# A chunked recurrence inside a two-block transformer kernel: crossed block products, convolution taps on two other engines, and three moved steps

## The reference

```python
y = _rwkv7_scan(stack(rh, rh), stack(w_f, w_b), stack(k_f, k_b), stack(vh, vh),
                stack(-kk, -kk), stack(b_f, b_b)).swapaxes(0, 1)
...
def _conformer_conv(u, dw_w, dw_b, ln_g, ln_b):
    h = u[..., :CV_WIDTH] * jax.nn.sigmoid(u[..., CV_WIDTH:])
    h = lax.conv_general_dilated(h, dw_w[:, None, :], (1,), [(CV_CONV_LEN // 2, CV_CONV_LEN // 2)],
                                 dimension_numbers=('NWC', 'WIO', 'NWC'),
                                 feature_group_count=CV_WIDTH) + dw_b
    return jax.nn.silu(_layernorm(h, ln_g, ln_b))
```

## Time and profile before

| | us |
|---|---|
| median of three runs | 2925.84 (2919.92 to 2928.39) |
| the profiled execution | 2918.31 |
| its span in the trace | 2916.2 |
| chunk loop of layer 0, first product of group 0 to the end of group 3 | 288.78 to 399.60 |
| chunk loop of layer 1 | 1054.24 to 1156.00 |

### The profile page before, as it was taken

One profiled execution on the slowest core, in us unless ns is written; L12 is line 12 of the kernel. 1 busy time (PEld: TensorE's weight loads), 2 busy tenths in 40 slices (PEclk: granted clock), 3 DMA queues, 4 the chain that ended last, 5 costly groups with the idle time before them and its releaser, 6 DMA issues.

```text
span 2916.2 us, 50739 instructions
## 1 busy us (share of the span) xinstructions
PE 2723.9 (93%) x21324; PEld 2292.6 (79%) x21324; DVE 1932.3 (66%) x2283; ACT 1478.5 (51%) x1753; POOL 103.4 (4%) x79
## 2 busy tenths in 40 slices
PE   6998888999999978799999999999999789989999
PEld 4875876888768767778878787887877779987999
DVE  3365865322454666488888888888888657665766
ACT  3345243222334433377677677767776445443544
POOL 1100000000013000100000000000000000000000
PEclk9998999999999999899999999999999889999999
DMA  8514101322234230189899898989996424542453
GB/s 320 220 58 168 74 3 58 116 88 101 91 130 170 86 125 4 40 333 371 336 348 352 334 367 335 369 337 349 364 346 258 163 102 174 188 149 87 159 188 116
DMA packets 81796, 581.69 MB, mean 199 GB/s; under 512 B 9272, under 2 KB 11072, under 8 KB 11840
## 3 DMA queue, kind: packets, MB, share of 16 engines
q1 hardware_dynamic: 78336, 571.48, 52.2%
q10 hardware_dynamic: 3264, 7.33, 0.7%
HBM read 577.73 MB, written 1.05 MB: 198 GB/s over the span
## 4 chain that ended last, share of the span: by engine, by line
PE 81%; DVE 9%; ACT 4%; PEld 2%; issue 1%; DMA 1%; PEldq 1%; POOL 0%; POOLq 0%; ACTq 0%; DVEq 0%; SPq 0%
PE banks L2496 20%; PE banks L2520 11%; PE banks L1077 8%; PE banks L857 8%; PE banks L2836 8%; PE banks L1103 3%; PE banks L891 3%; PE banks L3164 3%; PE banks L1540 3%; PE banks L2088 1%; DVE ring_split L307 1%; PEld banks L679 1%; DVE ring_split L2673 1%; PE banks L522 1%; DVE x_buf L2662 1%
## 5 line engine op out<-in xcount | busy, mean ns | idle before, releaser
L2673 DVE TENSOR_TENSOR ring_split<-ring,arena_split 128x2048 fp32r<-128x2048 f32 x336 | 768.2, 2291 | 90.9 <-ACT arena_split L2601 83.2
L2601 ACT ACTIVATE arena_split<-ring 128x2048 fp32r<-128x2048 f32 x336 | 644.4, 1919 | 52.3 <-PE banks L2520 52.3
L307 DVE TENSOR_TENSOR ring_split<-ring,arena_split 128x2048 fp32r<-128x2048 f32 x144 | 331.1, 2301 | 346.4 <-ACT arena_split L301 346.4
L301 ACT ACTIVATE arena_split<-ring 128x2048 fp32r<-128x2048 f32 x144 | 274.4, 1908 | 104.4 <-PE banks L1077 74.0
L2496 PE MATMUL banks<-arena_split 128*128 128x512 f32 x896 | 300.7, 398 | 11.7 <-DVE ring_split L2673 11.7
L2496 PE MATMUL banks<-arena_split,mix_split 128*128 128x512 f32 x896 | 304.2, 401 | 6.4 <-DVE ring_split L2673 6.4
L2520 PE MATMUL banks<-arena_split 128*128 128x512 f32 x896 | 297.4, 392 | 1.0 <-DVE arena_split L2702 1.0
L2496 PEld LDWEIGHTS banks<-arena_split 128*128 128x128 f32 x896 | 169.1, 189 | 48.8 <-DVE ring_split L2673 13.4
L2496 PEld LDWEIGHTS banks<-arena_split,mix_split 128*128 128x128 f32 x896 | 168.3, 188 | 45.0 <-DVE ring_split L2673 8.3
L2520 PEld LDWEIGHTS banks<-arena_split 128*128 128x128 f32 x896 | 168.2, 188 | 43.2 <-issue 4.0
L857 PE MATMUL banks<-mix_split,ring_split 128*128 128x256 f32 x704 | 199.0, 283 | 0.0
(11 more groups left out here) (408 smaller groups left out, 5431.9 us busy)
## 6 DMA issues: line engine op xcount, KB each, us to landing
ring<-parts SPq DMA_DIRECT2D x541, 1024.0 KB, 4.8
arena<-bias ACTq DMA_DIRECT2D x2, 2048.0 KB, 9.7
x_buf<-xt SPq DMA_DIRECT2D x1, 2048.0 KB, 7.8
constants<-con SPq DMA_DIRECT2D x1, 1952.0 KB, 14.5
out<-x_buf ACTq DMA_DIRECT2D x4, 256.0 KB, 2.2
arena<-lora ACTq DMA_DIRECT2D x2, 256.0 KB, 3.2
arena<-gate ACTq DMA_DIRECT2D x2, 256.0 KB, 3.5
arena<-sgw ACTq DMA_DIRECT2D x2, 256.0 KB
```

Of the source, the lines that this page charges most:

```text
L301: act.activation(high[:, m % depth, :], slots[:, n % RING, :], ACT.Copy).then_inc(w_high.h, w_high.one(times))
L307: dve.tensor_tensor(low_slots[:, n % RING, :], slots[:, n % RING, :], high[:, m % high.shape[1], :].bitcast(F32), ALU.subtract).then_inc(w ...
L2601: act.activation(high[:, m % 3, :], slots[:, m % RING, :], ACT.Copy).then_inc(wh_ok.h, 1)
L2673: dve.tensor_tensor(low_slots[:, m % RING, :], slots[:, m % RING, :], high[:, m % 3, :].bitcast(F32), ALU.subtract).then_inc(wl_ok.h, 1)
```

## The change

It has five parts.

1. **Crossed block products.** D2T.D2, D2.E, D2.D2T, D4T.D4, D4.E, LL.E and E.LL (steps p2, p3, p5) go through `crossed`, which puts the second direction's output into the other partition half and into the next bank. What is added to E (`E + D2.E`, `E + D4.E`) can no longer be added by VectorE, because E lies in the old half, so `plus=True` adds E on TensorE, as a product with the identity into the same accumulation; VectorE then copies. The order of blocks in DD, DT, LL, E changes from step-first to direction-first. `apply` (the two solves) crosses too.
2. **Taps.** In layer 0, channel tile 0, VectorE keeps taps 0 to 15 (16 instructions). All the others become a product on ScalarE (`Taps.products`) into a small ring of buffers and an addition on GpSimd (`Taps.sums`): 45 of 512 columns in layer 0, with 2 buffers; 60 of 256 columns in layer 1, with 4. ScalarE waits for GpSimd when the ring is full.
3. **The next group's `dl`** runs on TensorE between `solve(s, 1)` and `p7`, and VectorE masks it (`grams_out`) ahead of `g`. `bs` now waits for the mask `l` of the next group.
4. **Low weight halves.** The first is cut in four quarters that VectorE does inside group 3; the second moves into the tail, behind the first state update. ScalarE's high halves stay.
5. **The ring of tap buffers** lies over three tables that only the second block uses (`cos`, `sin`, `sel`, 1024 columns, 512 KB). They are no longer loaded at the start, but by SyncE ahead of the experts' first weights. `kb1` moves from before p3 to before p4.

The core of the diff:

```diff
+        def products(self, act, count):
+            made, added = S("cv_part"), S("cv_tap")
+            for n in range(self.made, min(self.made + count, len(self.units))):
+                i, t = self.units[n]
+                if n >= len(self.parts):
+                    act.wait_ge(added.h, added.at(n - len(self.parts) + 1))
+                act.activation(self.parts[n % len(self.parts)], self.source(i, t), ACT.Copy, scale=Q1(self.l, "cv_w", 2 * t + i))\
+                    .then_inc(made.h, made.one())
...
+        def sums(self, pool):
+            for n, (i, t) in enumerate(self.units):
...
+                pool.wait_ge(made.h, made.at(n + 1))
+                pool.tensor_tensor(self.acc[i], self.acc[i], self.parts[n % len(self.parts)], ALU.add).then_inc(added.h, added.one())
...
+            def crossed(b, k, left, right, plus=False):
+                o = [bank(b + d)[:, k * 256:(k + 1) * 256].rearrange("p (i t) -> p i t", i=4) for d in range(2)]
+                for i in range(4):
+                    for w in range(2 if plus else 1):
+                        for d in range(2):
+                            for h in hs:
+                                to = hs[1 - hs.index(h)] if d else h
+                                mm = pe.matmul(o[d][to, i, :], eye[h, 0, :] if w else left[h, 4 * d + i, :], right[h, 4 * d + i, :],
+                                               start=w == 0, stop=w == int(plus))
...
-                products(b8(0), D2T, D2)
-                products(b8(1), D2, D2T)
-                products(b8(2), D2, E[g % 2]).then_inc(P_.h, P_.one(f"p2_{g}"))
+                crossed(0, 0, D2T, D2)
+                crossed(0, 1, D2, E[g % 2], plus=True)
+                pe.wait_ge(V_.h, V_.at(f"km0_{g}"))
+                crossed(2, 0, D2, D2T).then_inc(P_.h, P_.one(f"p2_{g}"))
                 if g:
                     solve(s, 0)
-                pe.wait_ge(V_.h, V_.at(f"km0_{g}"))
-                against_zr(kt, g, 1).then_inc(P_.h, P_.one(f"kb1_{g}"))
...
-                products(b8(0), D4T, D4)
+                crossed(2, 0, D4T, D4)
                 pe.wait_ge(V_.h, V_.at(f"e2_{g}"))
-                products(b8(1), D4, E[g % 2]).then_inc(P_.h, P_.one(f"p3_{g}"))
+                crossed(0, 0, D4, E[g % 2], plus=True).then_inc(P_.h, P_.one(f"p3_{g}"))
                 if g:
                     state(s, 0)
+                pe.wait_ge(A_.h, A_.at(f"d8_{g}"))
+                against_zr(kt, g, 1).then_inc(P_.h, P_.one(f"kb1_{g}"))
...
-                products(b8(0), LL, E[g % 2])
-                products(b8(1), E[g % 2], LL).then_inc(P_.h, P_.one(f"p5_{g}"))
+                crossed(2, 0, LL, E[g % 2])
+                crossed(0, 0, E[g % 2], LL).then_inc(P_.h, P_.one(f"p5_{g}"))
...
                 if g:
                     solve(s, 1)
+                if g + 1 < NG:
+                    grams(g + 1)
...
+                if g + 1 < NG:
+                    pe.wait_ge(V_.h, V_.at(f"l_{g + 1}"))
                 turned((0, 1), 0, lambda h, q, cs: bt[h, q, cs], g).then_inc(P_.h, P_.one(f"bs_{g}"))
...
+                taps.products(act, 2 if taps.own else 2)
+                pair_out("n", "p5", g, 0, N1)
...
-                if g >= NG - 2:
-                    split_low(dve, out_high, out_first + g - (NG - 2), 2 + g - (NG - 2))
...
                     state(NG - 1, 0)
+                    split_low(dve, out_high, out_first + 1, 3)
...
+            late = slice(CON["cos"][0], CON["sel"][1])
+            sp.dma_start(con[:, late], con_in[:, late]).then_inc(S("rotation_loaded").h, 16)
```

More of the change, by code:

```diff
@@ new lines, in begin @@
+        def begin(self, act):
+            first = S("cv_begun")
+            for i in range(1 if self.own else 0, 2):
+                act.activation(self.acc[i], self.source(i, 0), ACT.Identity, scale=Q1(self.l, "cv_w", i), bias=Q1(self.l, "cv_b", i))\
+                    .then_inc(first.h, first.one())
+        def products(self, act, count):
[6 more added lines that the diff above has]
+                    .then_inc(made.h, made.one())
+            self.made = min(self.made + count, len(self.units))
@@ L1667, in _ @@
                 mm.then_inc(P_.h, P_.one(f"dl_{g}"))
+            grams(0)
+            for g in range(NG):
+                s = g - 1
                 if g:
@@ L1824, in _ @@
                 fill_act(act, g, "zb")
+                taps.products(act, 1 if taps.own else 2)
                 out("d2t", "p1", g, 2, D2T)
@@ L1828, in _ @@
                 fill_act(act, g, "p1")
-                out("d4t", "p2", g, 1, D4T)
+                taps.products(act, 2 if taps.own else 3)
+                pair_out("d4t", "p2", g, 2, D4T)
                 if g:
@@ L1838, in _ @@
                 fill_act(act, g, "p4")
-                out("n", "p5", g, 1, N1)
+                taps.products(act, 2 if taps.own else 2)
+                pair_out("n", "p5", g, 0, N1)
                 if g:
@@ L1842, in _ @@
                 fill_act(act, g, "p5")
-                out("n2", "p6", g, 3, N2)
+                taps.products(act, 1 if taps.own else 2)
+                out("n2", "p6", g, 4, N2)
                 if g:
@@ L1952, in _ @@
                 after(f"p2_{g}")
-                copy(D4, b8(0), f"d4_{g}")
-                add(e, b8(2), e, f"e2_{g}")
+                copy(pair_like(D4), pair(0, 0), f"d4_{g}")
+                copy(pair_like(e), pair(0, 1), f"e2_{g}")
+                taps.some(dve, 1)
+                after(f"p3_{g}")
+                copy(pair_like(e), pair(0, 0), f"e3_{g}")
+                if g:
+                    state(s, 0)
                 after(f"kb1_{g}")
@@ L1957, in _ @@
                 taps.some(dve, 1)
[L1958 to L1963 removed]
+                if g == NG - 1:
+                    quarter_low(0)
                 after(f"p4_{g}")
                 own()
[L1966 removed]
+                add(e, b8(0), e, f"e4_{g}")
                 taps.some(dve, 1)
+                if g == NG - 1:
+                    quarter_low(1)
                 after(f"p5_{g}")
[L1969 to L1970 removed]
+                copy(pair_like(NTb), pair(2, 0), f"nt_{g}")
+                add(pair_like(INT_), pair(2, 0), eye_pair, f"int_{g}")
+                if g + 1 < NG:
+                    grams_out(g + 1)
+                else:
+                    quarter_low(2)
+                    quarter_low(3)
                 taps.some(dve, 2)
```

139 lines of the change are left out of this document (87 added, 52 removed).

## The result

| | us |
|---|---|
| the kernel before, median of 12 runs | 2924.66 (2918.43 to 2929.32) |
| the changed kernel, median of 12 runs | 2931.88 (2925.17 to 2939.85) |
| ratio changed to before, 95% interval | 1.0023 (1.0014 to 1.0032), +6.7 us |
| its profiled execution, span | 2939.85, 2938.0 |

What follows compares the result with a forecast made beforehand. No one engine bounds it: a relay of TensorE batches and copies does. Layer 0 4.0 + layer 1 6.0 + stall 8.4 - GpSimd contention 5 = 13.4, rounded to 14 us: median 2925.8 to 2912, range 2901 to 2924 (forecast's own 2906 to 2917).

Steps and rivals of the forecast that it cites:

- The price of a crossed product: Matmul records using all four quadrants: 17 ns each taken, 22 as a bound, 30 as the worst; uncrossed 30 to 31.
- The legs: Start-to-start steps in both loops: gains of 4.0 us in layer 0 and 6.0 us in layer 1.
- p3's reader to p4: Leg in each group: 0.74 us becomes 1.1 behind `kb1`, a loss of 0.4, or 0.15 in layer 0.
- p4 to p5: Leg of 2.45 us in layer 1, TensorE's own work 2.0: gain 0.4 in groups 1 and 2; 0 where outputs run.
- reader to p6: Leg after p5: 0.75 us both ways if ScalarE's `n` is punctual; `n` 0.5 late in layer 0, 0.1 in layer 1.
- The early `dl`: From p6 onwards: replaces TensorE idle time, so gains nothing; `bs` waits at most 0.3 us for the mask `l`.
- The stall at group 3: Group 3 of both layers: TensorE's wait during VectorE's low half and the lower clock after it go, gain 8.4 us.
- GpSimd against VectorE: Both loops: the engines stop each other, costing 4 us in layer 0 and 1 in layer 1; loss 5, between 0 and 13.
- Rival 3: GpSimd becomes the bound, slower: +65 us, so 2990, or just beyond the point +12, so 2938; chance 0.09.
- Moved constants: At the start and ahead of the experts: 512 KB less or more to load where TensorE does not wait, 0.
- Rival 4: Crossed pairs that accumulate run at 30 ns in p2 and D4.E: +5 us, so 2931; about -4 at 25 ns; chance 0.08.
- A sign that was named: In the loops: a lower granted clock because TensorE idles more between shorter batches would show the forecast wrong; no size given.

## Why the prediction was wrong, step by step

- **The price of a crossed product** (17 ns) was right for a batch, p5's 1.23 us against 1.26. Taken for what a record costs the kernel it was wrong: the added E costs 33 ns a record. That is the first step that failed: p2 as 128 records x 17 ns + 0.2, and D4.E plus E in 1.06, with no term for a wait on the instruction stream. The forecast had p2, p3 and kb1 at a gain of about 5 us. Measured, part 1 without its p5 loses 12.
- **The legs.** p2 from start to reader took 2.59 (L1, with a gap in it; 2.35 forecast), p3's reader came 3.69 after p2's instead of 2.6, with a gap of 0.83 in D4.E. p3's reader to p4 was 1.13, as forecast. p4 to p5 took 2.87 instead of 2.05, again with a gap; reader to p6 0.75, as forecast, and `n` was not late.
- **The early `dl`** ("so it gains nothing", at most 0.3 for the mask) is the second step that failed, and costs about as much: 6.4 us in the changed kernel, 9.4 alone. I looked at TensorE's idle time and wrote of `g` "about 1 late" only for group 1 of layer 0, at no more than 1 us. The wait was 2.03, and the lower clock came behind it. That the wait causes the lower clock is not shown. For it: with the own taps behind `g` both are gone from that place. Against a plain rule: in the run of part 3 alone the wait of 1.85 us in group 2 of layer 0 was followed by 8.6 us at the full clock (below, that run's window, columns as in the earlier trace rows), and before the change group 1 of layer 0 began at the lower level with no wait longer than 1.21 us ahead of it.

```profile
372.40:381.00 8.60, 4.88 (x184) 4.50 (x186) 7.28 (x12) 3.23 (x5) 0.00 (x0) 1.00 0.01 2
```

- **The stall at group 3.** The mechanism was right, to the number: p2 starts 4.85 us into group 3 in both layers (382.30 - 377.45 and 1147.08 - 1142.23), where about 5 was forecast. The size came out smaller: 8.4 forecast, 5.0 (1.8 to 8.2) measured alone. In that run's profile, group 3 of layer 1 is 4.0 us shorter, near its share of the forecast, and that of layer 0 only 1.7, although D4's copy is 3.7 us earlier in it than before; with taps on VectorE, quarters stand ahead of the state update and of `g`.
- **GpSimd against VectorE.** Loss 5 forecast; taps and ring together cost 2.9 (-0.6 to 6.4), with VectorE's relief in it, so the contention by itself has no measured price. Additions of 1.35 us (mean, layer 0) and 0.75 (layer 1) were as forecast. Rival 3 (GpSimd the bound) fell: ScalarE waited 0.9 us for it in all.
- **Moved constants**: from the phase behind layer 1's loop to the end, the run with the taps alone took 1739.7 us against 1740.3 before. Nothing, as forecast.
- **Rival 4** (2931) met the time by luck: accumulating pairs do not run at 30 ns, they run at 17 and then wait. Its estimate for 25 ns a record was also wrong as a sum: p2 and D4.E, reckoned as the rival reckons them, lose 1.5 us a group against the legs, 12 in all, which leaves -2, not -4.
- **A sign that was named** came true: a lower granted clock in the loops was on the list of what would show the forecast wrong, and groups 1 and 2 of layer 1 had 0.94. The forecast gave it no term.

What stays open: the parts do not add up. Alone they are +7.0, +2.9, +9.4 and -5.0, together 14.3, and the changed kernel is +6.7. With five intervals of about 3 us on either side, the shortfall of 7.6 is itself only just clear of noise (some 7, an estimate). Taking part 1 out of it changed nothing, taking part 3 out gave 6.4. Both make TensorE wait in the same groups, so one wait may cover the other, but no run here shows that. Nor does the sum of stream waits alone give the time: the changed kernel without part 3 has 27.8 us of them (1.2 of it no block's end) and is as fast as before.

## What to carry to other kernels

Where small matmuls already follow each other at 30 ns, count records as well as engine time: look for idle time that ends on "issue" in the middle of a batch, at equal distances in records. Crossing a batch was worth about its leg where it added no record (p5); records that are added to a crossed batch are not paid for at the batch's rate. And a step that is moved into another engine's idle time must be followed on the engine that reads its result: what stands in that queue, and who waits behind it.

## What was not expected of the hardware

- TensorE's instructions arrive in blocks of some 127 matmul records with their weight loads. From one block's end with a gap to the next it was never less than 3.5 us in the changed kernel's loops, and 3.3 at the least in any run, so that four-quadrant batches (17 ns a record) were cut by gaps of up to 2.0 us, 26 us in two loops. In all 24 gaps the next record came 1.2 to 1.5 us after a 16384-byte packet had landed.
- Behind waits of about 2 us the next group's first batch often ran at the lower clock level, some 3.1 us for 62 records instead of 2.02, but not always. Over both loops and their tails the lower level was granted for 48 us in the changed kernel's profile, its slowest execution, and 25 in that of before; over all 16 kernels' profiles it was 7 to 48, one execution each. How much of the changed kernel's time is the clock is not known.
